# First stage of a two-block transformer kernel: two weight chunks and the input transferred by halves in order of use, early low parts on VectorE, squares and token sums later

## The reference

```python
u = rmsnorm(h, norm_in[i])      # x * rsqrt(mean(x*x) + EPS) * norm_in
proj = u @ w_in[i]
(m_q, m_k, m_v, m_o, m_z, m_if, a_q, a_k, a_v, a_z,
 ix_q, ix_k, ix_w) = jnp.split(proj, SPLIT_POINTS, axis=-1)
...
sc = jax.nn.relu(jnp.einsum('bthd,bsd->bths', iqb, ik))
score = jnp.einsum('bths,bth->bts', sc, iwb).astype(jnp.float32)
_, idx = lax.top_k(score, topk)
```

## Time and profile before

| what | value |
|---|---|
| median of 3 runs | 1614.32 us (1612.59 to 1614.68) |
| profiled execution | 1613.07 us |
| its span, first to last instruction | 1611.3 us |
| PE matmul busy | 1590.6 us (99%) |
| DVE, ACT, POOL busy | 1006.9, 741.2, 658.0 us |

### The profile page before, as it was taken

The page is one execution under the profiler, slowest core; times in us unless marked ns, Lnnn a source line. Parts: engine busy times, 40 slices in busy tenths (PEclk is TensorE's granted clock), DMA queues, the critical chain, the costliest instruction groups (busy, mean ns, idle before and its releaser), DMA issues.

```text
span 1611.3 us, 22075 instructions
## 1 busy us (share of the span) xinstructions
PE 1590.6 (99%) x7779; PEld 1266.0 (79%) x7779; DVE 1006.9 (62%) x1631; ACT 741.2 (46%) x1287; POOL 658.0 (41%) x307
## 2 busy tenths in 40 slices
PE   7999999999999999999999999999999999999999
PEld 6688767777888888777778888787788888888887
DVE  6699586677337877777785056665586765566100
ACT  5423465565345555655553255454534444434220
POOL 4344563333454245344464332222254354444442
PEclk9999999999999999999999999999999999999999
DMA  6243322214333235211123322121333233333331
GB/s 213 80 118 92 92 79 66 66 53 143 92 105 98 60 107 173 79 53 53 53 67 92 92 66 66 53 66 53 112 100 97 79 105 94 102 91 103 93 98 59
DMA packets 40363, 143.38 MB, mean 89 GB/s; under 512 B 4494, under 2 KB 5166, under 8 KB 39894
## 3 DMA queue, kind: packets, MB, share of 16 engines
q1 hardware_dynamic: 37600, 131.96, 27.2%
q10 hardware_dynamic: 2678, 10.27, 1.9%
HBM read 137.63 MB, written 4.58 MB: 88 GB/s over the span
## 4 chain that ended last, share of the span: by engine, by line
PE 84%; issue 9%; POOL 3%; DVE 3%; ACT 1%; DMA 0%; POOLq 0%; DVEq 0%; ACTq 0%
PE bank L800 18%; PE bank L802 18%; PE bank L801 18%; PE bank L1461 4%; PE bank L1462 4%; PE bank L1463 4%; POOL w_lo L660 2%; PE bank L1347 2%; PE bank L852 1%; PE bank L853 1%; PE bank L851 1%; PE bank L1368 1%; PE bank L1356 1%; PE bank L1254 1%; PE bank L1260 1%
## 5 line engine op out<-in xcount | busy, mean ns | idle before, releaser
L660 POOL TENSOR_TENSOR w_lo<-w_raw,w_hi 128x1024 fp32r<-128x1024 f32 x241 | 589.7, 2450 | 917.5 <-ACT w_hi L1491 780.1
L800 PE MATMUL bank<-u_hi,w_hi 128*128 128x512 f32 x768 | 323.8, 422 | 2.5 <-ACT gm L2046 2.5
L1491 ACT ACTIVATE w_hi<-w_raw 128x1024 fp32r<-128x1024 f32 x197 | 207.3, 1056 | 210.7 <-PE bank L802 169.5
L802 PE MATMUL bank<-u_hi,w_lo 128*128 128x512 f32 x768 | 300.6, 391 | 0.0
L801 PE MATMUL bank<-u_lo,w_hi 128*128 128x512 f32 x768 | 299.7, 390 | 0.0
L800 PEld LDWEIGHTS bank<-u_hi,w_hi 128*128 128x128 f32 x768 | 144.4, 188 | 46.3 <-issue 13.5
L802 PEld LDWEIGHTS bank<-u_hi,w_lo 128*128 128x128 f32 x768 | 144.1, 188 | 31.4
L801 PEld LDWEIGHTS bank<-u_lo,w_hi 128*128 128x128 f32 x768 | 144.6, 188 | 30.3 <-issue 2.4
L1461 PE MATMUL bank<-u_hi,w_hi 128*128 128x512 f32 x288 | 112.0, 389 | 0.0
L1462 PE MATMUL bank<-u_lo,w_hi 128*128 128x512 f32 x288 | 112.0, 389 | 0.0
L1463 PE MATMUL bank<-u_hi,w_lo 128*128 128x512 f32 x288 | 112.0, 389 | 0.0
(11 more groups left out here) (484 smaller groups left out, 3394.2 us busy)
## 6 DMA issues: line engine op xcount, KB each, us to landing
w_raw<-weights SPq DMA_DIRECT2D x243, 512.0 KB, 3.6
xt<-x_t SPq DMA_DIRECT2D x8, 256.0 KB, 6.4
hank<-bias_dram ACTq DMA_DIRECT2D x8, 256.0 KB, 4.6
xt<-x_t ACTq DMA_DIRECT2D x1, 2048.0 KB, 8.6
h_dram<-h_res ACTq DMA_DIRECT2D x1, 2048.0 KB, 7.7
h_res<-h_dram ACTq DMA_DIRECT2D x1, 2048.0 KB, 7.5
out<-h_res SPq DMA_DIRECT2D x8, 256.0 KB
p_val<-p_t ACTq DMA_DIRECT2D x1, 512.0 KB, 10.8
```

Source lines behind the costliest of these rows:

```text
L660: pool.tensor_tensor(w_lo[:, j, :], w_raw[:, j, :], w_hi[:, j, :].bitcast(F32), ALU.subtract).then_inc(w_lo_ready, 1)
L800: pe.matmul(o, hi, xh, start=(i == 0), stop=False)
L802: mm = pe.matmul(o, lo, xh, start=False, stop=(i == n - 1))
L1491: act.activation(w_hi[:, c % RING, :], w_raw[:, c % RING, :], ACT.Copy).then_inc(w_hi_ready, 1)
```

## The change

It touches the first stage only.

- SyncE transfers W0 and W1 in two halves of 512 columns each, in the order first half of W0, x0, x1, first half of W1, x2, x3, second half of W0, x4, x5, second half of W1, x6, x7. Twelve transfers stand where ten stood, ahead of the constants and W2.
- ScalarE makes the high parts in the same order. Its first activation is now the copy of W0's first half, then the root function's first call (`load_root`), then the rest. The transfer of `squares_f` is issued after x3. Then comes W2's high part, and only after it the eight squares, then W3's high part.
- VectorE makes all twelve low parts in that order, the weights' ones too; the six additions of squares come after all of them, and so does the wait for `squares_f`. GpSimd starts with W2's low part, after waiting for the low parts of W0 and W1.
- PE first runs six float32 matmuls (`WARM`) of `ones` with `ones` into bank 7, as soon as `ones` is set. Then it takes the parts in order of arrival: `q0` with x0 and x1, `q1` with x0 and x1, then both in turns. The token sums stand after the first four eighths of `q2`, the spread after the other four.

```diff
+        early = [("first half", 0), ("x", 0), ("x", 1), ("first half", 1), ("x", 2), ("x", 3), ("second half", 0),
+                 ("x", 4), ("x", 5), ("second half", 1), ("x", 6), ("x", 7)]
 # SyncE
-            for j in range(2):
-                sp.dma_start(w_raw[:, j, :], a["weights"][j]).then_inc(w_landed[j], 16)
-                for i in range(4 * j, 4 * j + 4):
+            for kind, i in early:
+                if kind == "x":
                     sp.dma_start(xt[:, i, :], a["x_t"][:, i, :]).then_inc(x_in[i], 16)
+                elif kind == "first half":
+                    sp.dma_start(w_raw[:, i, 0:S], a["weights"][i][:, 0:S]).then_inc(half_landed[i], 16)
+                else:
+                    sp.dma_start(w_raw[:, i, S:], a["weights"][i][:, S:]).then_inc(w_landed[i], 16)
 # GpSimd
-            low_parts(0, index_chunks[0])
+            pool.wait_ge(w_lo_ready, 2)
+            low_parts(2, index_chunks[0])
 # TensorE
+            pe.wait_ge(ones_ready, 1)
+            for _ in range(WARM):
+                pe.matmul(bank[7][:, :], ones[:, 0:P], ones[:, :], start=True, stop=True)
+            for j, k in ((0, 0), (0, 1), (1, 0), (1, 1)) + tuple((j, k) for k in range(2, KD) for j in range(2)):
+                pe.wait_ge(xg_lo_ready, early_parts.index(("x", k)) + 1)
+                column_tile((q0, q1)[j], of_xg, part=(k, k + 1),
+                            weights=early_parts.index(("first half", j)) + 1 if k < 4 else None)
+            column_tile(q2, of_xg, part=(0, 4))
+            token_sums(lambda k: sq[:, 0, :], lambda k: sq[:, 1, :])
+            column_tile(q2, of_xg, part=(4, 8))
             spread_scale(0, 5)
-            column_tile(q2, of_xg, part=(1, 8))
 # ScalarE
+            early_high(*early[0])
             act.wait_ge(vecs_in, 16)
             load_root()
+            for kind, i in early[1:]:
+                early_high(kind, i)
+                if (kind, i) == ("x", 3):
+                    act.dma_start(squares_f[:, :], a["squares_f"]).then_inc(squares_in, 16)
+            next_hi[0] = 2
+            split_weights(2 - RING)
             for i in range(KD):
-                if i % 4 == 0:
-                    split_weights(i // 4 - RING)
-                act.activation(xg_hi[:, i, :], x_tile(i), ACT.Copy, scale=vec("norm_in", i)).then_inc(xg_hi_ready, 1)
                 square_part(i, xt[:, i, :], sq[:, 0, :], u_val, sq[:, 1, :])
             split_weights(-1)
 # VectorE
+            for kind, i in early:
+                if kind == "second half":
+                    dve.wait_ge(w_hi_ready, i + 1)
+                    early_weight_low(i, slice(S, 2 * S))
+                    continue
+                dve.wait_ge(xg_hi_ready, early_parts.index((kind, i)) + 1)
+                if kind == "x":
+                    dve.scalar_tensor_tensor(xg_lo[:, i, :], xt[:, i, :], vec("norm_in", i), xg_hi[:, i, :].bitcast(F32),
+                                             ALU.mult, ALU.subtract).then_inc(xg_lo_ready, 1)
+                else:
+                    early_weight_low(i, slice(0, S))
             dve.wait_ge(squares_in, 16)
+            for i in range(1, KD - 1):
+                add_part(sq[:, 0, :], u_val[:, (i - 1) % 2, :], i == 1)
```

More of the change, by code:

```diff
@@ L38 @@
 RING = 4
+WARM = 6
 VEC = {}
@@ L355, in build @@
         w_landed = [sem(f"w_landed{i}") for i in range(RING)]
+        half_landed = [sem(f"half_landed{i}") for i in range(2)]
         w_hi_ready = sem("w_hi_ready")
@@ L425, in build @@
         x2_ready = sem("x2_ready")
-        v_tok_ready = sem("v_tok_ready")
         norm_sums_in = sem("norm_sums_in")
@@ L618, in build @@
         block = ctx.enter_context(nc.Block())
+        early = [("first half", 0), ("x", 0), ("x", 1), ("first half", 1), ("x", 2), ("x", 3), ("second half", 0),
+                 ("x", 4), ("x", 5), ("second half", 1), ("x", 6), ("x", 7)]
+        early_parts = [e for e in early if e[0] != "second half"]
         index_chunks = (st["idx_k"][0]["parts"][0][0], st["idx_k"][0]["upto"])
@@ L783, in open_bank, with column_tile @@
                     pe.wait_ge(freed[e], n)
-            def column_tile(t, rhs, ready=None, part=None, lows=lo_ready):
+            def column_tile(t, rhs, ready=None, part=None, lows=lo_ready, weights=None):
                 n = len(t["parts"])
@@ L793, in column_tile @@
                     c, s = t["parts"][i]
-                    if i == first or t["parts"][i - 1][0] != c:
+                    if weights is not None:
+                        pe.wait_ge(xg_lo_ready, weights)
+                    elif i == first or t["parts"][i - 1][0] != c:
                         pe.wait_ge(w_lo_ready, c + 1)
@@ L1570, in _, with early_high @@
             act.dma_start(vecs[:, :], a["vecs"]).then_inc(vecs_in, 16)
[L1571 to L1575, removed]
+            def early_high(kind, i):
+                if kind == "x":
+                    act.wait_ge(x_in[i], 16)
+                    act.activation(xg_hi[:, i, :], xt[:, i, :], ACT.Copy, scale=vec("norm_in", i)).then_inc(xg_hi_ready, 1)
+                elif kind == "first half":
+                    act.wait_ge(half_landed[i], 16)
+                    act.activation(w_hi[:, i, 0:S], w_raw[:, i, 0:S], ACT.Copy).then_inc(xg_hi_ready, 1)
+                else:
+                    act.wait_ge(w_landed[i], 16)
+                    act.activation(w_hi[:, i, S:], w_raw[:, i, S:], ACT.Copy).then_inc(w_hi_ready, 1)
+            early_high(*early[0])
             act.wait_ge(vecs_in, 16)
             load_root()
+            for kind, i in early[1:]:
[4 more added lines that the diff above has]
+            split_weights(2 - RING)
             for i in range(KD):
-                if i % 4 == 0:
-                    split_weights(i // 4 - RING)
-                act.activation(xg_hi[:, i, :], x_tile(i), ACT.Copy, scale=vec("norm_in", i)).then_inc(xg_hi_ready, 1)
                 square_part(i, xt[:, i, :], sq[:, 0, :], u_val, sq[:, 1, :])
@@ L2289, in _, with early_weight_low @@
             dve.wait_ge(vecs_in, 16)
-            dve.wait_ge(squares_in, 16)
[L2291 to L2296, removed]
+            def early_weight_low(j, half):
+                dve.tensor_tensor(w_lo[:, j, half], w_raw[:, j, half], w_hi[:, j, half].bitcast(F32),
+                                  ALU.subtract).then_inc(w_lo_ready if half.start else xg_lo_ready, 1)
+            for kind, i in early:
[4 more added lines that the diff above has]
+                dve.wait_ge(xg_hi_ready, early_parts.index((kind, i)) + 1)
+                if kind == "x":
+                    dve.scalar_tensor_tensor(xg_lo[:, i, :], xt[:, i, :], vec("norm_in", i), xg_hi[:, i, :].bitcast(F32),
+                                             ALU.mult, ALU.subtract).then_inc(xg_lo_ready, 1)
+                else:
+                    early_weight_low(i, slice(0, S))
+            dve.wait_ge(squares_in, 16)
+            for i in range(1, KD - 1):
+                add_part(sq[:, 0, :], u_val[:, (i - 1) % 2, :], i == 1)
             scales()
```

## The result

| | kernel before | changed kernel |
|---|---|---|
| median of 12 runs | 1612.88 us (1612.47 to 1614.68) | 1617.84 us (1615.23 to 1619.64) |
| profiled execution: span | 1611.3 us | 1616.4 us |

The change makes the kernel **0.29% slower**: the ratio is 1.0029 with a 95% interval of 1.0021 to 1.0037. The forecast was no change, 1614.2 us in a range up to 1616.5. The three runs of the kernel before that were shown first had their median 1.4 us above that of all twelve.

A forecast was written before the change was run, and what follows sets the result against it. PE, busy 1590.6 of 1611.3 us, bounds the kernel, with VectorE 0.45 us ahead at line 891. Of 3.9 us won, 0.1 stays: 1613.07 becomes 1613.0, plus 1.25 gives 1614.2 us, range 1610.4 to 1616.5.

The forecast's parts named there:

- PE's start: First stage on PE: real work starts effectively at 9.4 us instead of 13.3, 3.9 us won; bounds 6.7 to 11.7.
- effective start: When PE's real matmuls would have begun at 0.23 us each; 13.3 us before, 9.4 forecast.
- The second table load: ScalarE's start: root table may load behind the first copy, 1.28 us, hidden by six matmuls; the skill says about 2.66.
- The sums: Token sums on PE: start at 23.2 us, by PE and VectorE alike; 23.00 before.
- W2's landing: W2's transfer ahead of ScalarE's squares: lands at 15.6 us, uncertainty +0.5.
- Rival B: Six matmuls at PE's start too long, clock not released: 1616.5, or 1618.9 with slow real matmuls; chance 0.12.
- From the sums to `r_in`: Sums 1.7, four eighths of `q2` 2.9, spread to `r_in` 1.1 us; `r_in` at 28.9, 0.9 later than before.
- The u chain: `r_in` to the end of VectorE's line 2321: 21.4 us instead of 22.0, ending at 50.3.
- the three holds and the idling: VectorE's u chain: `u_lo` 3 held 1.1, `u_lo` 4 1.6, idling 1.2, W8's low part 1.1, atop 16.4 work.
- the two waits of PE: PE waits about 1.8 us in `att_q` tile 0's last step and 1.6 us ahead of line 891.
- Behind the transposes: From line 891 on nothing changes, so the 0.1 us left there is left at the end.
- The base: 1.25 us added to 1613.0, as the median of the runs stood that far above the profiled execution.

The follow-up runs named there:

- experiment 3: Changed kernel with squares 0 to 4 ahead of W2's high part on ScalarE; 1618.65 us, 1.0036 to the kernel before.
- experiment 5: Changed kernel with `u_hi` 7 made right behind `u_hi` 6, ahead of W8 and W9; 1614.6 us, 1.0011 to the kernel before.
- experiment 6: Changed kernel with W2 and W3 transferred ahead of the three constants; 1615.87 us, 1.0014 to the kernel before.
- experiment 7: Changed kernel: `u_hi` 7 before W8/W9, W2/W3 before constants, squares 0 and 1 before W2's high part, `squares_f` wait after additions, spread after two eighths; 1610.48 us.
- experiment 2: Changed kernel without its six matmuls of ones (`WARM = 0`); 1616.84 us, 1.0026 to the kernel before.
- experiment 1: Changed kernel with float32 filler matmuls (three, four, three) in front of PE's three late waits; 1614.42 us, 1.0011 to the kernel before.
- experiment 4: Kernel before with only PE's order changed: sums after four eighths of `q2`, spread after the other four; 1618.4 us, 1.0032.
- experiment 9: The kernel of experiment 7 with one filler matmul ahead of the token sums; 1609.82 us, 0.9983 to the kernel before.

## Why the prediction was wrong, point by point

**PE's start: right.** The effective start was 9.45 us (9.4 was worked out), the clock rose during the matmuls of ones, and real work ran at the high level from there. That the number came out to 0.1 us is partly chance: with the same six matmuls the first real one is at 9.05 us here and at 8.01 to 8.56 us in the profiles of experiments 3, 5, 6 and 7. The second table load came, 5.34 to 6.62 us, behind ScalarE's first copy. The root's call started at 6.64, with no drain to be seen, so the 2.66 us that the Trainium skill (ScalarE: Activation LUTs, "What ACT_TABLE_LOAD costs") gives for a switch are not what this place paid; 1.28 us are, and they were hidden.

**The sums: mis-sized by 1.1 us.** They started at 24.33, not 23.2. W2's landing, at 16.1, was 0.5 us later than I took, the upper end of my bound. The additions followed at 0.80 us, the upper end of 0.6 to 0.8, not 0.65 to 0.7. In the sum both stood at their low side, so PE, which I had arriving together with them, waited 1.1 us. Rival B's rule, that each us of a later start moves the sums one for one, didn't hold either: in experiment 2 PE came 1.1 us later and the sums started at 24.34 all the same, since VectorE's additions end at 24.1 to 24.3 us in either kernel.

**From the sums to `r_in`: the step that failed.** The prediction had every matmul behind the start at the high level, 0.23 us each, and gave the clock no term here. I put 1.7 + 2.9 + 1.1 = 5.7 us. It took 7.3 us, because the clock was low from 27.5 to about 31. In experiment 1, with the same sums at 24.37, it was 5.7 us, as worked out.

**The u chain: right.** 21.4 us were worked out, 21.2 measured here and in experiments 2 and 4. The sum is a little better than its parts: the three holds and the idling were put at 1.1, 1.6, 1.1 and 1.2 us and came out at 0.8, 1.8, 0.9 and 1.2. The collision of `u_lo` 4 with W7's low part, the idling of 1.2 us before `u_lo` 7 (1.20 in the row) and its meeting with W8's low part are all there, and so are the two waits of PE, 1.81 and 1.00 us against 1.8 and 1.6. Experiment 5 took 2 us out of it at the place named. The Trainium skill's lock (SBUF — State Buffer, "Who interferes with whom") held in each of these rows: GpSimd had begun first, and `u_lo` ended 0.55 us after it. My reading of the earlier trace rows for the other direction was too neat. There GpSimd began at 12.89, ahead of VectorE's addition at 13.05, and yet it was GpSimd that took 0.7 us too long, while the addition took its usual 0.68; another two-input instruction of VectorE had been running since 12.39. "Who issues first" doesn't describe that row.

```profile
12.39 0.74 DVE L2293 SCALAR_TENSOR_TENSOR xg_lo<-xt,vecs,xg_hi 128x512 fp32r<-128x512 f32 x1
```

**Behind the transposes: the second place where it failed.** I wrote that what is left at line 891 is left at the end. But PE's two waits let the clock fall there too, until 58 us, 2.6 us more. I had named the waits and their lengths, and the profile had shown in rows 3 what low-clock matmuls cost; I priced a wait at its length alone. Rival B had the low clock in it, at the wrong place: ahead of the work and not behind the waits. No rival had a clock that falls again later.

The terms add up: 1.1 (sums) + 1.6 (clock before `r_in`) - 0.2 (chain) and some rounding make the transposes 2.6 us later than forecast, 2.6 us (clock behind them) come on top, 5.2 us; the span of 1616.4 us is 5.2 above the 1611.2 that the forecast means.

**The base: chance.** I added 1.25 us because the median of three runs stood above the profiled execution. Two of the three happened to be slower ones; over twelve runs the median is 0.2 us below the profiled execution. So 1614.2 stands 1.4 us too high as a forecast of no change, and the distance to the measured 1617.84, 3.6 us, looks smaller than the 5 us that the steps missed.

What stays open: what exactly makes the clock fall. Waits of 1.1, 1.92, 1.81 and 1.85 us were followed by a fall, also one of 0.30 and one of 0.41 us near the sums; the 1.48 us in experiment 5 weren't, nor the 1.05 us at 683 us in the changed kernel, though the same wait was in experiment 1. So the length of a wait by itself doesn't decide it. The experiments show that in this stage the falls go when the waits go (1 and 2); what a wait needs besides, to bring a fall, they don't show.

The spread of the changed kernel's times, 4.4 us between lowest and highest against 2.2 us before, goes with the clock: the twelve runs from 1615.2 to 1619.6 us have mean granted clocks that fall step by step from 0.999 to 0.996. In the rounds of the experiments nearly all runs of the kernel before fall into two groups, 1612.5 to 1613.4 us at 1.000 and 1614.1 to 1614.6 at 0.999. Its one profile is of the first group, so where the clock fell in the second isn't shown.

## What to carry to other kernels

A wait on TensorE costs its length and, if the clock falls after it, the slow matmuls behind it too: here 1.6 us behind a wait of 1.1, 2.6 us behind 2.8, and 1.1 us behind one of 0.30. Where work is moved so that PE arrives early at something that another engine makes, check first whether that engine can be early too; an engine 0.45 us ahead of PE, as VectorE was at the transposes, is the next bound. The time won at the start became worth something only when `r_in` was moved forward and its chain shortened, and then through the halves and the order rather than the matmuls of ones.

## What the runs showed of the hardware that was not expected

- Waits of one to two us were often followed by the low clock for 3 to 6 us, starting as much as 3 us after the wait: the sums' wait ended at 24.33 and the low rate began near 27.5. Not always: behind 1.48 us (51.72, experiment 5) the clock was 1.00.
- The clock fell behind a wait of only 0.30 us when it was followed by 16 one-column matmuls (22.44 us, experiment 7; 0.57 between 25 and 27). In the kernel before the same sums without a wait had no fall, 23.00 to 27 us.
- A filler of one 128x256 float32 matmul ahead of those sums went with a clock of 1.00 in the profile of experiment 9, and in eight of its eleven runs the mean granted clock was 1.000 (four of eleven in experiment 7). The other three, at 0.999, took 1611.9 to 1612.0 us.
